# Moving the heads of q and k by DMA and VectorE block transposes instead of TensorE transposes

## The reference

```python
q = (rms_norm(c_q, q_lat_g) @ w_uq).reshape(B, S, MLA_HEADS, QK_DIM)         # 16 heads of 96
k = jnp.concatenate([k_nope, k_rope], axis=-1)                               # 64 of the head, 32 shared
q = rms_norm(q, q_norm_g)
k = rms_norm(k, k_norm_g)
q = jnp.concatenate([q[..., :QK_NOPE], apply_rope(q[..., QK_NOPE:], cos, sin)], axis=-1)
k = jnp.concatenate([k[..., :QK_NOPE], apply_rope(k[..., QK_NOPE:], cos, sin)], axis=-1)
s = jnp.einsum('bqhd,bkhd->bhqk', q_blk, k, preferred_element_type=jnp.float32) * scale
```

## Time and profile before

| what | us |
|---|---|
| median of 3 runs | 1437.53 |
| the profiled execution | 1437.35 |
| its span in the trace | 1435.6 |
| TensorE busy | 1425.4 (99%) |
| VectorE busy | 1164.2 (81%) |
| ScalarE busy | 959.6 (67%) |
| GpSimd busy | 46.2 (3%) |

### The profile page before, as it was taken

How to read it: one execution, slowest core, us unless ns; L and a number is a source line. 1 busy time by engine, 2 the same in 40 slices (tenths; PEclk the granted TensorE clock), 3 DMA queues, 4 the chain that set the end, 5 groups by cost and what they waited for, 6 DMA issues and landing times.

```text
span 1435.6 us, 19231 instructions
## 1 busy us (share of the span) xinstructions
PE 1425.4 (99%) x6747; PEld 1177.4 (82%) x6747; DVE 1164.2 (81%) x1184; ACT 959.6 (67%) x1002; POOL 46.2 (3%) x54
## 2 busy tenths in 40 slices
PE   9999999999999999999999999999999999999998
PEld 7888788888888888778888888888888888888886
DVE  6987756665547977766999999999999999999997
ACT  6676754544436676754677787777777777777775
POOL 2000003000000000000300000000000000000200
PEclk9999999999999999999999999999999999999999
DMA  9473348955465463447899999999999999999994
GB/s 338 158 239 118 118 155 304 334 177 178 159 214 185 149 233 117 141 153 282 288 374 415 384 358 408 376 386 409 364 397 383 377 413 369 386 387 400 372 397 172
DMA packets 163268, 415.13 MB, mean 289 GB/s; under 512 B 15421, under 2 KB 43961, under 8 KB 163177
## 3 DMA queue, kind: packets, MB, share of 16 engines
q1 hardware_dynamic: 157128, 393.42, 74.5%
q0 software_dynamic: 5008, 16.97, 3.5%
q10 hardware_dynamic: 1040, 3.68, 0.6%
HBM read 398.20 MB, written 15.81 MB: 288 GB/s over the span
## 4 chain that ended last, share of the span: by engine, by line
PE 92%; DVE 3%; ACT 2%; DMA 1%; POOL 1%; issue 1%; SPq 0%; DVEq 0%; ACTq 0%; POOLq 0%
PE ps L551 85%; PE ps L1095 1%; PE ps L825 1%; DVE w_lo L511 1%; POOL x_rows L797 1%; PE ps L968 1%; DMA x_rows<-xn,row_i 1%; ACT w_hi L506 1%; PE ps L947 1%; PE ps L955 1%; ACT qk_t L1238 1%; PE ps L934 0%; PE ps L903 0%; PE ps L946 0%; DMA raw<-in_w_in 0%
## 5 line engine op out<-in xcount | busy, mean ns | idle before, releaser
L511 DVE TENSOR_TENSOR w_lo<-raw,w_hi 128x2048 fp32r<-128x2048 f32 (+3 forms) x240 | 499.2, 2104 | 131.4 <-ACT w_hi L506 130.4
L506 ACT ACTIVATE w_hi<-raw 128x2048 fp32r<-128x2048 f32 (+3 forms) x240 | 421.9, 1770 | 187.7 <-PE ps L551 173.4
L551 PE MATMUL ps<-w_hi,act_hi 128*128 128x512 f32 (+1 forms) x1264 | 333.6, 392 | 0.8 <-ACT act_hi L1238 0.6
L551 PE MATMUL ps<-w_hi,act_lo 128*128 128x512 f32 (+1 forms) x1264 | 331.2, 388 | 0.0
L551 PE MATMUL ps<-w_lo,act_hi 128*128 128x512 f32 (+1 forms) x1264 | 328.3, 388 | 0.5 <-DVE w_lo L511 0.5
L551 PEld LDWEIGHTS ps<-w_lo,act_hi 128*128 128x128 f32 x1264 | 235.0, 188 | 50.5 <-DVE w_lo L511 2.9
L551 PEld LDWEIGHTS ps<-w_hi,act_lo 128*128 128x128 f32 x1264 | 234.9, 188 | 47.6
L551 PEld LDWEIGHTS ps<-w_hi,act_hi 128*128 128x128 f32 x1264 | 232.3, 188 | 47.6 <-ACT act_hi L1238 1.4
L511 DVE TENSOR_TENSOR w_lo<-raw_more,w_hi 128x2048 fp32r<-128x2048 f32 (+1 forms) x96 | 201.7, 2110 | 25.0 <-ACT w_hi L506 24.9
L506 ACT ACTIVATE w_hi<-raw_more 128x2048 fp32r<-128x2048 f32 (+1 forms) x96 | 170.0, 1776 | 55.2 <-PE ps L551 54.3
L506 ACT ACTIVATE w_hi<-raw_low 128x2048 fp32r<-128x2048 f32 (+1 forms) x64 | 115.9, 1810 | 36.3 <-PE ps L551 35.5
(11 more groups left out here) (284 smaller groups left out, 1257.5 us busy)
## 6 DMA issues: line engine op xcount, KB each, us to landing
raw<-in_moe_w_gu SPq DMA_DIRECT2D x128, 512.0 KB, 9.3
raw_more<-in_moe_w_down SPq DMA_DIRECT2D x80, 512.0 KB, 7.4
raw<-in_w_in SPq DMA_DIRECT2D x72, 512.0 KB, 4.7
raw_low<-in_moe_w_gu SPq DMA_DIRECT2D x64, 512.0 KB, 10.6
raw_more<-in_moe_w_gu SPq DMA_DIRECT2D x64, 512.0 KB, 10.6
raw<-in_moe_w_gu SPq DMA_DIRECT2D x64, 384.0 KB, 6.5
raw<-in_moe_w_down SPq DMA_DIRECT2D x48, 512.0 KB, 6.8
raw<-in_dense_w_gu SPq DMA_DIRECT2D x44, 512.0 KB, 5.0
```

The lines of the kernel that those rows point to most:

```text
L506: nc.scalar.activation(w_hi[:, self.split_slot(j), 0:n], self.raw(j)[:, 0:n], ACT.Copy).then_inc(self.hi, 1)
L511: nc.vector.tensor_tensor(w_lo[:, c, 0:n], self.raw(j)[:, 0:n], w_hi[:, c, 0:n].bitcast(F32), ALU.subtract).then_inc(self.lo, 1)
L551: return nc.tensor.matmul(dst, a, b, start=start and n == 0, stop=stop and n == 2)
```

## The change

q and k of a layer are turned in one go instead of by pairs. `qb` and `kb` become [128, 2, 3 groups of 32 columns, 16 heads, 32]. GpSimd's queue moves each 32-partition part of them to the 32 partitions of its group of columns: 12 DMAs for 8 heads of q or of k, 48 in a layer, 64 KB each. VectorE transposes the moved data in 32x32 blocks, in place: one instruction of 96x2048 for 8 heads (step `blocks`). For q ScalarE then copies the blocks with the gain to where the scores read them. k is read where it lies, in pieces of 32 columns. The steps are put into the plan like this, and `turn` steps are gone:

```diff
         mul(l, "ukv", 0, 0, [evac("ukv", 0)])
+        plan.append(("q_rope", l, 0))
         mul(l, "ukv", 1, 0, [evac("ukv", 1)])
-        plan.append(("head_sums", l, "k", 0))
-        mul(l, "ukv", 2, 0, [evac("ukv", 2)])
+        plan.append(("q_rope", l, 1))
+        mul(l, "ukv", 2, 0, [("head_sums", l, "k", 0), evac("ukv", 2)])
         mul(l, "ukv", 3, 0, [evac("ukv", 3)])
         plan.append(("head_sums", l, "k", 1))
+        plan.append(("k_scale", l, 0))
         mul(l, "ga", 0, 0, [("mix_tokens", l, 0)])
-        plan.append(("q_rope", l, 0))
+        plan.append(("k_scale", l, 1))
+        plan.append(("blocks", l, "q", 0))
         mul(l, "ga", 0, 4, [("mix_tokens", l, 1), evac("ga", 0)])
-        plan.append(("q_rope", l, 1))
+        plan.append(("blocks", l, "q", 1))
         mul(l, "u", 0)
-        plan.append(("k_scale", l, 0))
-        mul(l, "u", 0, 4, [("u_arg", l, 0), ("split", l, len(chunks)), ("u_gelu", l, 0)], split=False)
-        mul(l, "u", 1, 0, [("branch", l, 0), *slot(1, exps=False)], inside=[(4, turn(0))], split=False)
+        plan.append(("blocks", l, "k", 0))
+        mul(l, "u", 0, 4, [("u_arg", l, 0), ("split", l, len(chunks)), ("u_gelu", l, 0), ("blocks", l, "k", 1)], split=False)
+        mul(l, "u", 1, 0, [("branch", l, 0), *slot(1, exps=False)], split=False)
...
```

GpSimd:

```diff
+                def move_heads(to, src, half, moved):
+                    hs = slice(8 * half, 8 * half + 8)
+                    for b in range(4):
+                        for g in range(DG):
+                            pool.dma_start(to[half][32 * g:32 * g + 32, b:TT * 4:4, :, :], src[32 * b:32 * b + 32, :, g, hs, :]
+                                           ).then_inc(moved[half], 16)
+
+                pool.wait_ge(q_ready, TT * (l + 1))
+                for half in range(2):
+                    move_heads(q_blocks, qb, half, q_moved)
+                pool.wait_ge(lo_done, lent_read[l] + 1)
+                pool.wait_ge(k_ready, 2 * l + 1)
+                move_heads(k_blocks, kb, 0, k_moved)
+                pool.wait_ge(k_ready, 2 * l + 2)
+                for half in range(2):
+                    pool.wait_ge(q_moved[half], 16 * 4 * DG * (l + 1))
+                move_heads(k_blocks, kb, 1, k_moved)
```

TensorE, in the step `scores`, and ScalarE and VectorE in the step `blocks`:

```diff
-                    wait_turn_read(pe, qk_turn[l, pair])
-                    wait_turn_read(pe, qk_turn[l, pair] + 1)
+                    if pair % 4 == 0:
+                        pe.wait_ge(q_scaled, 2 * l + pair // 4 + 1)
+                        pe.wait_ge(k_turned, 2 * l + pair // 4 + 1)
...
+                elif kind == "blocks":
+                    if step[2] == "q":
+                        half = step[3]
+                        act.wait_ge(q_turned, 2 * l + half + 1)
+                        if not l and not half:
                             act.wait_ge(qk_gain_ready, 1)
+                        act.wait_ge(q_moved[1], 16 * 4 * DG * (l + 1))
+                        if half:
+                            for i in range(2):
+                                act.wait_ge(k_moved[i], 16 * 4 * DG * (l + 1))
+                        scale = qk_gain[0:DQ, l:l + 1]
+                        turned_blocks = q_blocks[half][0:DQ].rearrange("p b h i -> p h b i")
+                        for to, a in ((q_last, 0),) if half else ((q_first, 0), (q_second, 4)):
+                            n = to.shape[1]
+                            op = copy(to[0:DQ].rearrange("p h (b i) -> p h b i", i=32), turned_blocks[:, a:a + n], scale)
+                        op.then_inc(q_scaled, 1)
...
+                elif kind == "blocks":
+                    half = step[3]
+                    to, moved, done = (q_blocks, q_moved, q_turned) if step[2] == "q" else (k_blocks, k_moved, k_turned)
+                    dve.wait_ge(moved[half], 16 * 4 * DG * (l + 1))
+                    part = to[half][0:DQ].rearrange("p b h i -> p (b h i)")
+                    nc.vector.transpose(part, part).then_inc(done, 1)
```

```diff
+            def wait_slot(self, sp, e, j):
+                if user_before[j] is not None:
+                    sp.wait_ge(self.lo, user_before[j] + 1)
+                if j in keys_over:
+                    sp.wait_ge(scores_done, PAIRS * keys_over[j] + PAIRS // 2)
...
-                        flat = qb[:].rearrange("p t h d -> p t (h d)")
-                        op = copy(flat[:, :, j * STRIP:(j + 1) * STRIP], bank)
+                        n0, n1 = j * STRIP // 32, (j + 1) * STRIP // 32
+                        for g in range(DG):
+                            h0, h1 = -((g - n0) // DG), -((g - n1) // DG)
+                            at = DG * h0 + g - n0
+                            v = bank.rearrange("p t (n d) -> p t n d", d=32)[:, :, at:at + DG * (h1 - h0 - 1) + 1:DG, :]
+                            op = copy(qb[:, :, g, h0:h1, :], v)
...
-                    k = kb[:, :, heads, 0:DN]
-                    tt(k, k, ks.to_broadcast([P, TT, 8, DN]), ALU.mult)
+                    for g in range(DG - 1):
+                        k = kb[:, :, g, heads, :]
+                        tt(k, k, ks.to_broadcast([P, TT, 8, 32]), ALU.mult)
```

More of the change, by code:

```diff
@@ L221, in decoder_trunk @@
-        mul(l, "gb", 1, 4, [("split_lo", l, len(chunks) - 2), *slot(4, exps=False), ("k_scale", l, 1), split("split_lo"),
+                            ("branch", l, 1)], split=False, inside=[(4, ("u_tanh", l, 1))])
+        mul(l, "gb", 1, 4, [("split_lo", l, len(chunks) - 2), *slot(4, exps=False), split("split_lo"),
                             ("softmax", l, 3), evac("gb", 1)], split=False,
-            inside=[(2, ("exps", l, 2)), (5, ("a_turns", l, 1)), (7, turn(3)), (7, ("norm_probs", l, 2)),
+            inside=[(2, ("exps", l, 2)), (5, ("a_turns", l, 1)), (7, ("norm_probs", l, 2)),
@@ L224, in decoder_trunk @@
                     (7, split("split_hi"))])
         mul(l, "pa", 0, 0, [*slot(5, exps=False), split("split_lo"), ("softmax", l, 4)],
[L226 to L229, removed]
+            inside=[(4, split("split_hi"))])
+        mul(l, "pa", 0, 4, [*slot(6), evac("pa", 0)])
@@ L230, in decoder_trunk @@
+        mul(l, "ga", 1, 0, [*slot(7)])
+        mul(l, "ga", 1, 4, [*slot(8), evac("ga", 1)])
         mul(l, "pa", 1, 0, [("prob_turns", l, PAIRS - 1)], inside=[(4, ("values", l, PAIRS - 2))])
@@ L291, in decoder_trunk @@
         t1_lo = sb("t1_lo", [P, KD, S], F32R, mixer)
+        staged = ExitStack()
+        q_blocks = [sb(f"q_blocks{i}", [P, TT * 4, 8, 32], F32, staged) for i in range(2)]
+        staged.close()
         bt_hi = sb("bt_hi", [P, KD, S], F32R, mixer)
@@ L489, in load @@
                 elif self.n0 and j < RAW:
[L491 removed]
+                    sp.wait_ge(self.lo, last_users[j][0] + 1)
                 elif self.n0:
@@ L495, in load, with landings @@
                     wait_turn_read(sp, last_turn["merged_turns", L - 1, 1] - 1)
+            def load(self, sp, e, j, pieces):
+                self.wait_slot(sp, e, j)
                 for dst, src in pieces:
-                    sp.dma_start(dst, src).then_inc(self.landed[j % r], 16)
+                    sp.dma_start(dst, src).then_inc(self.landed[self.slot(j)], 16)
+            def landings(self, e, j):
+                r = len(self.slots)
+                return 32 * (j // r + 1) + 32 * (PER_EXPERT // r) * e
             def split_hi(self, act, e, j, n=CHUNK):
-                r = len(self.slots)
-                act.wait_ge(self.landed[j % r], 32 * (j // r + 1) + 32 * (PER_EXPERT // r) * e - self.short * (j % r < 2))
+                act.wait_ge(self.landed[self.slot(j)], self.landings(e, j))
                 if self.n0 + j >= SPLIT or not isinstance(e, int) or e > 0:
@@ L956, in _ @@
                                                      ident)
-                        mm.then_inc(turn_done, 1)
-                elif kind == "qk_turns":
-                    pair = step[2]
-                    if pair == 0:
-                        pe.wait_ge(q_ready, TT * (l + 1))
-                    if pair % 4 == 0:
-                        pe.wait_ge(k_ready, 2 * l + pair // 4 + 1)
-                    for hh in range(2):
-                        bank = turn_bank(b0 + hh)
-                        for q in range(4):
-                            src = (qb, kb)[q // 2]
-                            mm = nc.tensor.transpose(bank[0:DQ, q * P:(q + 1) * P], src[:, q % 2, 2 * pair + hh, :], ident)
                         mm.then_inc(turn_done, 1)
```

115 lines of the change are left out of this document (71 added, 44 removed).

## The result

The changed kernel takes 1461.31 us (median of 4 runs, 1459.66 to 1462.27) against 1437.35 beside it: 1.0164 times as long, 95% interval 1.0152 to 1.0176, or 24.0 us more. The forecast was 1458.5. One execution of all that are told of here was disturbed: 1777.23 us in experiment 2, at a granted clock of 0.751 where its others had 0.991 to 0.993; the ratio given there leaves it out.

What follows compares the result with a forecast made beforehand. TensorE, busy 1425.4 of 1435.6 us, was taken as the bound. 1437.35 + 17.8 (stalls less removed turns, both layers) + 3.2 (slow clock) + 0.2 = 1458.5 us; range 1438 to 1472.

Steps and rivals of the forecast that it cites:

- Stall A: TensorE waits 3.3 us for u 1's first chunk, whose rounding on ScalarE stands behind the wait for VectorE's q transpose.
- stall B: TensorE waits 7.4 us before scores 0, until VectorE's transpose of the first half of k ends at 130.4.
- C: TensorE waits 5.3 us before a_turns 0 for VectorE's branch step, delayed behind the second k transpose.
- TensorE's gain from the turns: Eight turn steps of 0.89 us leave TensorE in each layer: 7.1 us a layer, 14.2 in both.
- The rival "faster": The turns go and nothing is late: 1423.3 us; chance 0.14.
- 15 us to land: Argument that moves would not land late: the q groups have 15 us for landing.
- The clock, 3.2 us forecast: TensorE restarts at half rate after its waits, one slow start a layer: 2 x 1.6 = 3.2 us.
- rival 1: The same stalls with TensorE's clock unhurt: 1455.3 us; chance 0.2.
- Rivals 2 and 3: Moves land late before scores 0, 1470.5, chance 0.12; VectorE's instructions hold GpSimd's DMA issues, 1498, chance 0.03.
- The price of a packet: In GpSimd's DMA queue, a 1 KB packet costs between 0.05 and 0.16 us, nearer the lower.
- rival 2: Moves land late and set the wait before scores 0: 6 us a layer more, 1470.5; chance 0.12.
- The small edits: Extra evac uq copies, k read in 32-column pieces, one raw slot less: no cost taken; scores' bound 1 us a layer.

Runs made afterwards that it cites:

- experiment 2: Changed kernel with VectorE's block transpose of the second half of the keys moved from ahead of the branch step to behind slot 4: 1453.31 us, 1.0104.
- experiment 1: Changed kernel with ScalarE's two q steps (wait and copy) moved behind its roundings, VectorE and the moves as they were: 1440.18 us, 1.0018 times before.
- experiment 7: The reordered kernel (ScalarE's copies, moves and transposes placed anew) with nine of the twelve moves of q's second half issued earlier: 1425.07 us, 0.9915.
- experiment 5: Changed kernel with ScalarE copying only q_first at the first blocks step, q_second at the second: 1461.26 us, 1.0165.
- experiment 3: Changed kernel with throwaway transposes keeping TensorE busy in its three waits of a layer: 1458.00 us, 1.0138.
- experiment 4: The kernel before with the lending of the raw slot alone, turns still on TensorE: 1437.27 us, 0.9999.
- experiment 6: Changed kernel with three separate q copies, moves ordered q 0, k 0, q 1, k 1, transposes and steps around them moved: 1429.02 us, 0.9943.

## Why the prediction was right, and where its terms were off

**The mechanism.** Stalls A, B and C came at the three places, in both layers, by the releasers named (for B in layer 1 the trace names none). Ahead of them, one landing let ScalarE go in place of a transpose, and another was due beside one; both are told below. Putting ScalarE's two waiting steps behind its roundings takes 21.1 us off (experiment 1): that is the cause shown, not argued. TensorE's gain from the turns is as forecast: 6.2 us behind a_turns 0, and in experiment 7 the 14.2 of both layers are all there but for the waits named. The rival "faster" gave 1423.3 for turns gone and nothing late; that was its right price, and only another order of the work collects it.

**Stall A, +1.4 us in layer 0 and more in layer 1.** The forecast let ScalarE go at 110.7, when VectorE's transpose ends (111.0 measured). But its step writes q_second over the end of q's own tile, and so waits for all 24 moves of q. I had given the groups of q "15 us to land" and never set that landing beside the transpose. They were issued until 106.6 and let ScalarE go at 112.11, 1.4 after 110.7; in layer 1 at 553.70, 2.1 behind the transpose's end (551.57). With it a_turns 0 is 16.3 and 17.3 us late against 15.1: 3.4 us of the 3.8 by which the profiled execution is over the sum (24.9 against 21.15); the clock's term was 1.2 short, and some 0.7 us was made up again before the end. By experiment 5, however, this landing does not stand alone: without it the keys' landing takes its place. That VectorE's transpose decided stall B, as forecast, was therefore in part luck: had stall A been as short as forecast, B would have hung on the keys' landing, which I had at 121.5.

**Stalls B and C as waits.** TensorE waited 4.4 and 2.4 us where I wrote 7.4 and 5.3. The ends were nearly right (131.76 against 130.4, 139.62 against 138.4); what differs is that TensorE, at half rate, came to them later. I had put the half rate behind B and C only, but it was there from the first stall of 4.4 us on. It cost nothing there, by experiment 3.

**The clock, 3.2 us forecast.** Behind a_turns 0 it is 2.8 us in layer 0 and 1.6 in layer 1, 4.4 in the profiled execution; keeping TensorE busy takes 3.3 off the time. The sum needed this term, so rival 1 (1455.3) falls. By the Trainium skill (TensorE: Matmul & The Clock Gate, Why this matters for your kernels) an idle gap between bursts of matmuls throws the clock back to its lower level; the rows of 0.50 behind the waits agree. The granted clock of before, 1.00 throughout, was no evidence: that kernel had no such wait in it.

**Rivals 2 and 3.** The price of a packet was nearer its upper bound after all: the queue's time is 0.051 x 16 x 1460.5 = 1192 us now, less 0.035 x 16 x 1435.6 = 804, for 3072 more packets: 0.126 us each, where I had leaned to 0.05. The last moves of the keys had still landed by 123.27 (in experiment 5, issued 0.4 us later, at 123.71; in experiment 1 at 125.45), some 2 us later than the 121.5 that I had and far from the 6 of rival 2, since a group of 12 then takes 48 x 0.126 = 6.1 us, no more than its 6.4 of issue. VectorE did not hold GpSimd's issues: 24 in 12.85 us beside splits and scalings, 0.535 each, and 12 in 6.40 beside scalings and the block transpose that began at 108.70, 0.533 each, where it was 0.527 before.

```profile
93.73 12.85 POOL L833 DMA_DIRECT2D q_blocks<-qb  x24 [54.17 <-DVE qb L1713]
106.57 6.40 POOL L833 DMA_DIRECT2D k_lent<-kb  x12
```

**The small edits.** They cost nothing that shows. For the slot this is experiment 4. For the scores' reads, two matmuls of 128 columns take 0.38 or 0.39 us at full rate, as before, and from a slot's scores to the next 8.4 us pass, as the prediction has it (157.37 and 165.79 in experiment 6).

## What to carry to other kernels

Work taken from the bound engine is worth its price only if the steps that take its place stand, on their engines, behind what the bound engine needs next: look in each queue at what is behind a step that waits. Moving such a wait gave 21 us here, and shortening it gave none, because the next wait in line was already due. And the price of several stalls in a row is read at the last of them; here the slow clock cost time only behind that one.

## What was not expected of the hardware

**Landings under load.** From issue to landing a move of 64 KB took 5.7 us in the median for q and 6.2 for the first half of k, while the DMA share was 0.93 to 1.06. In experiment 7 the last group of k, issued from 119.75 on, took 2.2 in the median. The share was 1.05 from 115 to 119.75 and 0.55 from there to 130. The line is for the tile k_last in the trace of that kernel; in the changed kernel it is 3.1.

```profile
DMA to landing us min/median/max: 1.9/2.2/3.3
```

By the Trainium skill (DMA: Bandwidth & Descriptors, Anatomy of one DMA — SWDGE (gpsimd) path) a DMA of this queue takes 2.0 us plus its bytes over 436 thousand a microsecond, so by an estimate from that page 2.15 us for 64 KB. The last group agrees; in the busy stretch the time is nearly three times as long, where the forecast had gone by a landing after 2.8 us.

**The half rate behind the first wait.** I looked for it behind two stalls with little work between them. The rows have it behind the single wait of 4.38 us in layer 0 and that of 5.39 in layer 1, 3.75 us for eight matmuls in both; in experiment 5 eight behind a wait of 2.28 took 2.94.
